# Signalling the rotated differential queries and keys to TensorE in two parts instead of one

## The chip, the cores and the metric

The kernel runs on one core of one Trainium2 chip. The metric is the device time of one launch in microseconds (us). Three runs of the kernel before gave 2773.07, 2773.71 and 2776.54 us; the median is 2773.71 us.

The engines are called PE (TensorE, matrix products and transposes), PEld (its weight loads), DVE (VectorE), ACT (ScalarE), POOL (GpSimd) and SP (SyncE, which issues most DMAs).

## What is computed

Two blocks of two layers each work on a sequence of 512 rows of 1024 features. Only the first block is touched. In each of its layers a normed input `h` is multiplied with one wide matrix and cut into seven parts, of which `dq` and `dk` are the queries and keys of the differential attention:

```python
h = rmsnorm(x, g_mix[l])
dq, dk, dv, c_q, c_kv_kr, xq, gate_logits = jnp.split(h @ w_in[l], split_idx, axis=-1)
...
def diff_attention(q, k, v, ...):
    q = q.reshape(B, S, DIFF_HEADS, 2, DIFF_HEAD_DIM)      # 8 heads, 2 maps, 64 wide
    k = k.reshape(B, S, DIFF_HEADS, 2, DIFF_HEAD_DIM)
    q = rotary(rmsnorm(q, q_gain), c, s_)
    k = rotary(rmsnorm(k, k_gain), c, s_)
    o = causal_block_attention(q, k, v, DIFF_HEAD_DIM ** -0.5)
```

`dq` and `dk` are 1024 columns each. After the norm and the rotation they are needed with the features on the partitions, so the kernel turns them on TensorE (a transposition by a product with the identity). Beside the differential attention a layer has a latent attention (`mla`, fed by `c_q` and `c_kv_kr`) and an attention over a memory (`cross`), then gates, an output product and a feed-forward part.

## The kernel before

All products are in 32-bit floats and are made from parts: every weight slab of 128 rows is split into a high and a low part, and a product is three passes (high by high, low activations by high weights, high activations by low weights). SP loads the slabs into a ring of four. POOL writes the high part of a slab (line 371) and then the low part (line 374) into one of two places (`weight_parts`); for a few projections ACT writes the high parts (line 382). A place comes free when TensorE has used the slab that was in it. TensorE's product of a projection is `project`: for each slab it waits for the high part, makes two passes, waits for the low part, and makes the third (line 460 where the output has tokens on the partitions). Four matmuls are one pass. Every engine works through its own list in the order in which it is written; nothing is reordered.

The eight banks of PSUM are two halves of four, used in turn by the projections. `turn` (line 485) makes transposes into the half that the projection around it doesn't use, after the half has been emptied.

The columns of `dq` and `dk` are handled in four groups of 512 columns, called 0 to 3: `dq0`, `dq1`, `dk0`, `dk1`. For each group DVE does `products` (sums of squares at line 1381, the scaling at 1454, the four products with the rotation tables at 1458 to 1462, the reciprocal at 1466) and `sums` (the two sums at 1470 and 1471, the scaling with the norm at 1473, and a drain). Groups 0 and 1, and then group 2, are rotated while `dq1` to `dk1` are projected. Then DVE takes part in the eight units of the cross attention (`A.steps(0, U1, ...)`), and only behind these it rotates group 3. After group 3 comes a drain that raises the semaphore `diff_roped` once (line 1504).

On TensorE the eight cross units are woven into the projections `dk1` and `lat0`. Then comes the projection `lat1`: eight slabs of 336 columns. Ahead of its slabs 1, 3, 5 and 7 it calls `turn_diff(0)` to `turn_diff(3)`, which turn groups 0 to 3 into `d_t0` to `d_t3`, 16 transposes each. All four wait for `diff_roped` to be 1. `d_t0` also needs the half of PSUM that `lat0` filled; ACT empties that (line 1193). After each turn ACT copies the bank half to `qkt`, and the next turn waits for that copy.

After `lat1` come `dv0` (with two turns of the latent part in it), the small projections `qb0` to `kvb1`, `dv1`, and then the 32 units of the differential attention. DVE's next work after group 3 is the low parts of the turned latent rows (line 600), and later the rotation and norms of the latent attention (from line 1536).

Of the kernel before, what the change touches and what calls it, by code (L numbers as in the profile page):

```python
# [877 lines left out]
def block_one(nc, io, m, s, layer, prev):  # L878
# [106 lines left out]
    for p2 in range(CH // 2):  # L985
        for i in (0, 3, 1, 2):
# [3 lines left out]
                              v=[(lambda kb, h=h: mv[:, kb, h * CHD:(h + 1) * CHD]) for h in hh]))  # L990
    for h in range(DH):
        for i in (0, 3, 1, 2):
            units.append(dict(kind="diff", pair=h, i=i, n=(i + 1) * P, mask=(m["causal16"][:], i * P),
                              q=[qkt[r, h, i * P:(i + 1) * P] for r in halves], k=[qkt[r, 8 + h, 0:(i + 1) * P] for r in halves],
                              v=[(lambda kb, h=h: dv[:, kb, h * P:(h + 1) * P])], scaled=len(units) - U1 + 1, joined=lam_neg))
    for p2 in range(MH // 2):
        for i in (0, 3, 1, 2):
# [3 lines left out]
                              v=[(lambda kb, h=h: vm[:, kb, h, :]) for h in hh], first=True, last=True, bank=6 + p2 % 2,  # L1001
# [39 lines left out]
    if True:  # L1041
# [21 lines left out]
        def _(pe):  # L1063
# [34 lines left out]
                L.turn(pe, f"lat_t{k}", [(c % 4, t * P, lat_chunk(t, c)) for c in chunks for t in range(TT)])  # L1098

            def turn_diff(k):  # L1100
                pe.wait_ge(s["diff_roped"], 1)
                L.turn(pe, f"d_t{k}", [(c, t * P, qk[:, t, (4 * k + c) * P:(4 * k + c + 1) * P]) for c in range(4) for t in range(TT)])

            L.project(pe, "dq1", ht, {4: turn_xq, 6: turn_mk})
            L.project(pe, "dk0", ht)
            L.attend(pe, A, 0, U1, ("dk1", ht), ("lat0", ht), every=2)
            L.project(pe, "lat1", ht, {1 + 2 * k: lambda k=k: turn_diff(k) for k in range(4)})
            L.project(pe, "dv0", ht, {2: lambda: turn_latent(0), 4: lambda: turn_latent(1)})
            L.emptied(pe, "lat_t1")
# [249 lines left out]
        def _(dve):  # L1359
            v = nc.vector  # L1360
# [122 lines left out]
            A.maximum(0)  # L1483
            A.maximum(1)
            turning_of[2][1]()

            def finish(u):
                a = units[u]
                dve.wait_ge(s["weighted"], u + 1)
                r = m["recip"][:, u % 8, :]  # L1490
                v.reciprocal(r, m["rowsum"][:, u % 8, :])
                v.drain()
                sums = ps[:, 6 + u % 2, 0:2 * P]
                i, p2 = a["i"], a["pair"]
                if a["kind"] == "cross":
                    v.tensor_tensor(oc[:, i, 2 * p2 * P:2 * (p2 + 1) * P].rearrange("p (j d) -> p j d", j=2),
                                    sums.rearrange("p (j d) -> p j d", j=2), bc(r, [P, 2, P], 2),
                                    ALU.mult).then_inc(s["finished"], 1)
                    return
# [648 lines left out]
```

## Time and profile before

| what | value |
|---|---|
| device time, median of 3 runs | 2773.71 us |
| device time, lowest and highest | 2773.07 and 2776.54 us |
| span of the profiled execution, first to last instruction | 2772.1 us |
| mean granted TensorE clock | 0.980 of full speed |
| PE busy | 2606.5 us, 94% of the span |
| POOL busy | 1947.2 us, 70% |
| DVE busy | 1093.7 us, 39% |
| ACT busy | 770.6 us, 28% |

The profile is of one execution; the device time of that very execution is not among the three listed, and the median of the runs is 1.6 us above the profile's span. A busy share is an average over the whole program. The part that matters here is short: from about 208 us to 245 us of the span in the first layer, and the same stretch from about 1258 us in the second. Times in a row are from the start of the span. In a row of the timeline, "[8.37 <-DVEq L1504]" says that the engine was idle for 8.37 us before the row and that DVE's queue, at line 1504, ended the idle time. Rows merge equal instructions that follow each other, and the busy time of a merged row of matmuls overlaps the next row a little, so durations of stretches are taken from one start to the next.

### The profile page before, as it was taken

To read this page: it belongs to the slowest core of one execution; us is meant where nothing else is said; L and a number is where in the kernel's file an instruction comes from. 1 tells how busy PE (TensorE), PEld (TensorE's weight loads), DVE (VectorE), ACT (ScalarE), POOL (GpSimd) and SP (SyncE) were. 2 spreads that over 40 slices of the span, in tenths; PEclk is the share of its full clock that TensorE was granted. 3 is DMA by queue.
4 is the path that set the end of the run, shared out by engine and by line. 5 is a ranking of instruction groups with operands and counts; after the bars stand their busy time and mean duration, and the time that the engine had idled before them with its cause. 6 is when DMAs were issued, how large, how long until landed. Compare 5 with 4: busy or idle time off the path is not lost. (4 is left out here: it accounts for less than half of the span.)

```text
span 2772.1 us, 35631 instructions
## 1 busy us (share of the span) xinstructions
PE 2606.5 (94%) x13648; PEld 2108.8 (76%) x13652; DVE 1093.7 (39%) x1710; ACT 770.6 (28%) x1517; POOL 1947.2 (70%) x1604
## 2 busy tenths in 40 slices
PE   5998899999999999998899999999998997989987
PEld 4887677877878887787677878888887975688756
DVE  3544773111220112544674211210102399536883
ACT  4332474100120112342374100120111233313251
POOL 4646704888898888746803888898896878277844
PEclk9999999999999999999999999999999998999989
DMA  4322201333333333322201333233333431043202
GB/s 134 97 62 68 62 1 39 91 95 92 107 91 96 96 97 114 95 67 67 73 1 31 88 94 92 92 95 96 95 99 78 107 81 34 28 96 90 75 1 76
DMA packets 159257, 214.49 MB, mean 77 GB/s; under 512 B 51696, under 2 KB 69360, under 8 KB 159088
## 3 DMA queue, kind: packets, MB, share of 16 engines
q1 hardware_dynamic: 120336, 207.27, 25.7%
q10 hardware_dynamic: 38752, 4.95, 1.3%
q8 instruction: 109, 1.79, 0.3%
q14 instruction: 60, 0.49, 0.1%
HBM read 210.06 MB, written 2.10 MB: 77 GB/s over the span
## 5 line engine op out<-in xcount | busy, mean ns | idle before, releaser
L371 POOL TENSOR_TENSOR weight_parts<-weight_ring,zero 128x512 fp32r<-128x512 f32 (+4 forms) x730 | 789.2, 1081 | 667.9 <-PE ps L462 351.8
L374 POOL TENSOR_TENSOR weight_parts<-weight_ring,weight_parts 128x512 fp32r<-128x512 f32 (+3 forms) x804 | 1059.0, 1317 | 136.0 <-ACT weight_parts L382 77.9
L462 PE MATMUL ps<-h_feature_major_high,weight_parts 128*128 128x512 f32 x2304 | 588.9, 394 | 9.7 <-POOL weight_parts L371 9.4
L462 PEld LDWEIGHTS ps<-h_feature_major_high,weight_parts 128*128 128x128 f32 x2304 | 428.2, 188 | 115.7 <-POOL weight_parts L371 16.9
L460 PE MATMUL ps<-weight_parts,h_feature_major_high 128*128 128x512 f32 (+3 forms) x1904 | 429.4, 363 | 20.5 <-POOL weight_parts L371 7.8
L460 PEld LDWEIGHTS ps<-weight_parts,h_feature_major_high 128*128 128x128 f32 x1904 | 333.4, 189 | 72.9 <-POOL weight_parts L371 11.3
L462 PE MATMUL ps<-h_feature_major_low,weight_parts 128*128 128x512 f32 x1152 | 309.7, 391 | 0.0
L460 PE MATMUL ps<-weight_parts,ut_high 128*128 128x512 f32 x1008 | 251.6, 390 | 1.1 <-POOL weight_parts L371 0.9
L462 PEld LDWEIGHTS ps<-h_feature_major_low,weight_parts 128*128 128x128 f32 x1152 | 217.4, 189 | 46.0
L460 PE MATMUL ps<-weight_parts,h_feature_major_low 128*128 128x512 f32 (+3 forms) x952 | 227.3, 361 | 0.0
L460 PEld LDWEIGHTS ps<-weight_parts,ut_high 128*128 128x128 f32 x1008 | 188.3, 188 | 43.6 <-POOL weight_parts L374 2.2
L460 PEld LDWEIGHTS ps<-weight_parts,h_feature_major_low 128*128 128x128 f32 x952 | 169.8, 189 | 22.5
L825 ACT ACTIVATE probs<-ps,negmax 128x256 f32<-128x256 f32 (+3 forms) x320 | 164.2, 522 | 78.2 <-DVE negmax L811 77.2
L701 PE MATMUL ps<-arena 64*128 64x256 f32 (+8 forms) x640 | 154.7, 484 | 29.0 <-ACT probs L825 19.4
L1636 DVE TENSOR_TENSOR ut_low<-outs,ut_high 128x2048 fp32r<-128x2048 f32 x16 | 45.6, 2852 | 319.0 <-ACT ut_high L1355 319.0
L811 DVE TENSOR_REDUCE negmax<-ps 128x2 f32<-128x512 f32 (+3 forms) x160 | 129.2, 808 | 85.4 <-PE ps L706 62.2
L1351 ACT ACTIVATE outs<-ps 128x2048 f32<-128x2048 f32 x16 | 30.1, 1884 | 405.4 <-PE ps L462 405.4
L460 PE MATMUL ps<-weight_parts,ut_low 128*128 128x512 f32 x504 | 134.8, 389 | 0.0
L462 PE MATMUL ps<-ot_high,weight_parts 128*128 128x512 f32 x512 | 128.1, 389 | 0.0
L1326 ACT ACTIVATE arena<-ps,small 128x512 f32<-128x512 f32 x48 | 29.1, 689 | 319.8 <-PE ps L462 319.8
L701 PEld LDWEIGHTS ps<-arena 64*128 64x128 f32 (+2 forms) x640 | 67.6, 194 | 64.5 <-ACT probs L825 26.7
L462 PEld LDWEIGHTS ps<-ot_high,weight_parts 128*128 128x128 f32 x512 | 96.1, 188 | 19.9
(297 smaller groups left out, 3057.4 us busy)
## 6 DMA issues: line engine op xcount, KB each, us to landing
weight_ring<-in_w_in SPq DMA_DIRECT2D x272, 256.0 KB, 2.6
weight_ring<-in_w_mlp SPq DMA_DIRECT2D x256, 256.0 KB, 2.6
weight_ring<-in_w_out SPq DMA_DIRECT2D x64, 256.0 KB, 2.7
weight_ring<-in_w_mem_kv SPq DMA_DIRECT2D x32, 256.0 KB, 2.7
weight_ring<-in_w_diff_o SPq DMA_DIRECT2D x32, 256.0 KB, 2.6
weight_ring<-in_w_in SPq DMA_DIRECT2D x32, 170.0 KB, 2.3
weight_ring<-in_w_in SPq DMA_DIRECT2D x32, 168.0 KB, 2.2
weight_ring<-in_w_in SPq DMA_DIRECT2D x32, 163.0 KB, 2.2
```

The lines of the kernel that those rows point to most:

```text
L371: self.nc.gpsimd.tensor_tensor(high, raw, self.m["zero"][:].broadcast_to([P, raw.shape[1]]), ALU.add).then_inc(self.s["slab_high"], 1)
L374: self.nc.gpsimd.tensor_tensor(low, raw, high.bitcast(F32), ALU.subtract).then_inc(self.s["slab_split"], 1)
L460: last = self.nc.tensor.matmul(banks[:, t, 0:width], h[:, cut], w, **ends)
L462: last = self.nc.tensor.matmul(banks[:, t, :], w[:, cut], h, **ends)
L701: last = pe.matmul(bank[:, 0:a["n"]], a["q"][j], a["k"][j], start=True, stop=a["mask"] is None)
L811: last = dve.tensor_reduce(out, self.m["ps"][:, 2 * (u % 2):2 * (u % 2) + 2, 0:a["n"]], AX.X, ALU.max, negate=True)
L825: last = act.activation(self.m["probs"][:, u % 3, j, 0:a["n"]], self.m["ps"][:, 2 * (u % 2) + j, 0:a["n"]], ACT.Exp, bias=self.m["negmax"] ...
L1326: last = a.activation(gates[k % 2][:, j, :], L.banks(name)[:, j, :], ACT.Sigmoid, bias=bgate[:, ch:ch + 1])
L1351: a.activation(r, L.banks(f"up{f}{j}"), ACT.Relu)
L1636: v.tensor_tensor(ut[1][:, 4 * j:4 * j + 4, :], rect[(f * ups + j) % 2], ut[0][:, 4 * j:4 * j + 4, :].bitcast(F32), ALU.subtract).then_inc ...
```

## The change

The wait of the first three turns is unchanged in number, the wait of the fourth becomes 2, and DVE gets one more drain with a raise of the semaphore directly behind the rotation of group 2. So the first raise now says that groups 0 to 2 are done, and the old raise, behind group 3, is the second. No arithmetic, no transfer and no buffer is changed, and the order of work on every engine stays as it was. The change stands once in the code and works in both layers of the first block.

```diff
             def turn_diff(k):
-                pe.wait_ge(s["diff_roped"], 1)
+                pe.wait_ge(s["diff_roped"], 1 if k < 3 else 2)
                 L.turn(pe, f"d_t{k}", [(c, t * P, qk[:, t, (4 * k + c) * P:(4 * k + c + 1) * P]) for c in range(4) for t in range(TT)])
...
             A.maximum(0)
             A.maximum(1)
             turning_of[2][1]()
+            v.drain().then_inc(s["diff_roped"], 1)
 
             def finish(u):
```

## Rows read from the trace of the kernel before

**Rows 1.** The page, busy time and share of each engine.

```profile
PE 2606.5 (94%) x13648; PEld 2108.8 (76%) x13652; DVE 1093.7 (39%) x1710; ACT 770.6 (28%) x1517; POOL 1947.2 (70%) x1604
```

**Rows 2.** Line 1504: its drains, and who waited for them (us, times).

```profile
L1504 DVEq DRAIN  x2: 19/19/19, 221.0 to 1270.6; - x2
...
  PEld ps L485: 17.3, 2
```

**Rows 3.** PE timeline, first layer: start, us, engine, line, operation [idle before <-releaser].

```profile
211.77 0.89 PE L460 MATMUL ps<-weight_parts,h_feature_major_high 128*128 128x336 f32 x4 [0.27 <-POOL weight_parts L374]
221.03 3.68 PE L485 MATMUL ps<-ident,arena 128*128 128x128 f32 x16 [8.37 <-DVEq L1504]
...
229.06 1.91 PE L485 MATMUL ps<-ident,arena 128*128 128x128 f32 x16
230.72 0.86 PE L460 MATMUL ps<-weight_parts,h_feature_major_high 128*128 128x336 f32 x4
...
234.50 1.91 PE L485 MATMUL ps<-ident,arena 128*128 128x128 f32 x16
```

**Rows 4.** PE timeline, the same place in the second layer.

```profile
1261.38 0.89 PE L460 MATMUL ps<-weight_parts,h_feature_major_high 128*128 128x336 f32 x4 [0.27 <-POOL weight_parts L374]
1270.65 3.68 PE L485 MATMUL ps<-ident,arena 128*128 128x128 f32 x16 [8.38 <-DVEq L1504]
...
1277.91 0.82 PE L485 MATMUL ps<-ident,arena 128*128 128x128 f32 x6
```

**Rows 5.** ACT timeline: `lat0` is emptied.

```profile
209.94 1.30 ACT L1193 ACTIVATE probs<-ps 128x1344 f32<-128x1344 f32 x1 [1.52 <-PE ps L460]
```

**Rows 6.** DVE timeline, first layer.

```profile
177.58 0.69 DVE L811 TENSOR_REDUCE negmax<-ps 128x2 f32<-128x512 f32 x1 [6.43 <-PE ps L701]
...
211.03 1.77 DVE L1461 TENSOR_TENSOR arena<-arena,small 128x1024 f32<-128x1024 f32 x1
...
216.24 1.76 DVE L1471 TENSOR_TENSOR arena<-arena,outs 128x1024 f32<-128x1024 f32 x1
218.08 2.82 DVE L1473 TENSOR_TENSOR arena<-arena,small 128x2048 f32<-128x2048 f32 x1
252.15 2.73 DVE L600 SCALAR_TENSOR_TENSOR latt_low<-ps,small,latt_high 128x512 fp32r<-128x512 f32 x4 [31.25 <-ACT latt_high L593]
...
320.22 0.43 DVE L811 TENSOR_REDUCE negmax<-ps 128x2 f32<-128x256 f32 x1 [9.34 <-PE ps L706]
```

**Rows 7.** POOL timeline, slabs 1 to 3 of `lat1`, first layer.

```profile
211.68 1.72 POOL L371 TENSOR_TENSOR weight_parts<-weight_ring,zero 128x336 fp32r<-128x336 f32 x1
213.48 1.76 POOL L374 TENSOR_TENSOR weight_parts<-weight_ring,weight_parts 128x336 fp32r<-128x336 f32 x1
215.20 1.72 POOL L371 TENSOR_TENSOR weight_parts<-weight_ring,zero 128x336 fp32r<-128x336 f32 x1
217.00 1.75 POOL L374 TENSOR_TENSOR weight_parts<-weight_ring,weight_parts 128x336 fp32r<-128x336 f32 x1
227.53 0.75 POOL L371 TENSOR_TENSOR weight_parts<-weight_ring,zero 128x336 fp32r<-128x336 f32 x1 [8.77 <-PE ps L460]
228.35 0.92 POOL L374 TENSOR_TENSOR weight_parts<-weight_ring,weight_parts 128x336 fp32r<-128x336 f32 x1
```

**Rows 8.** DVE timeline, group 1 of the rotation, first layer.

```profile
143.97 3.22 DVE L1473 TENSOR_TENSOR arena<-arena,small 128x2048 f32<-128x2048 f32 x1
```

**Rows 9.** POOL timeline beside rows 8.

```profile
145.81 2.52 POOL L374 TENSOR_TENSOR weight_parts<-weight_ring,weight_parts 128x512 fp32r<-128x512 f32 x1 [0.78 <-ACT weight_parts L382]
148.53 1.29 POOL L374 TENSOR_TENSOR weight_parts<-weight_ring,weight_parts 128x512 fp32r<-128x512 f32 x1 [0.20 <-ACT weight_parts L382]
```

**Rows 10.** Windows: length, busy us of PE, PEld, DVE, ACT, POOL, then clock.

```profile
212.60:221.00 8.40, 0.06 (x1) 0.00 (x0) 8.15 (x6) 0.00 (x0) 6.00 (x4) 0.71 0.22 61
221.00:224.40 3.40, 3.37 (x17) 3.37 (x17) 0.00 (x0) 0.00 (x0) 0.00 (x0) 0.50 0.00 0
```

**Rows 11.** Windows: the start of the differential attention in both layers.

```profile
321.00:328.00 7.00, 4.01 (x29) 2.14 (x27) 6.02 (x12) 4.94 (x19) 7.00 (x6) 1.00 0.00 0
1370.00:1377.00 7.00, 5.03 (x28) 3.03 (x27) 6.38 (x12) 4.88 (x19) 7.00 (x5) 0.76 0.00 0
```

## The prediction, made before the changed kernel ran

> **What bounds the kernel now.** I read the page first: TensorE is busy 94% of the span [rows 1], so a time in which it stands still is a time that the program loses, unless something behind it is late anyway. Then the view of the line that raises the semaphore: TensorE's weight loads waited twice for line 1504, 17.3 us in all [rows 2]. Then TensorE's timeline around both waits. In the first layer the last pass of slab 0 of `lat1` starts at 211.77, and the first of the 16 transposes of `d_t0` only at 221.03, after 8.37 us of idle time that DVE's queue ended [rows 3]; in the second layer the same wait is 8.38 us [rows 4]. Last the timelines of the other engines in that stretch, to see what else TensorE would have had to wait for.
>
> **What the wait costs, with what follows it.** After the idle time TensorE runs at its lower level: the granted clock is 0.71 over the idle stretch and 0.50 (1.2 of 2.4 GHz) over the 3.4 us in which `d_t0` is made [rows 10]. So I don't take the idle time as the price but compare the stretch with an undisturbed one. At full clock, `d_t1` takes 230.72 - 229.06 = 1.66 us, and from its start to that of `d_t2` there are 234.50 - 229.06 = 5.44 us, so two slabs take 3.78, a slab 1.89 and a pass 0.63 [rows 3]. From the last pass of slab 0 to `d_t1` there would be 0.63 + 5.44 = 6.07 us without any wait. There are 229.06 - 211.77 = 17.29 in the first layer and 1277.91 - 1261.38 = 16.53 in the second [rows 3, 4] (the clock came back sooner there). Too much: 11.22 and 10.46, together 21.7 us.
>
> **What the change removes and adds.** Groups 0 to 2 were rotated before the cross attention, so their signal has long been given when TensorE comes to `d_t0`. What else must be there: the half of PSUM that `lat0` filled, which ACT has emptied at 209.94 + 1.30 = 211.24 [rows 5], before TensorE gets there at 211.77 + 0.63 = 212.40. So the first wait goes entirely. The fourth turn now waits for the second raise, at 218.08 + 2.82 = 220.9 in DVE's timeline [rows 6], and it comes to that place about 10 us later than this (below); that wait is free. The added drain stands between the rotation of group 2 and the cross attention. The drain of line 1504 takes 19 ns [rows 2], and DVE waits 6.43 us for TensorE soon after the new one [rows 6]; I take 0. Without that cover it would be some 0.02 us for each layer, or with a restart of DVE's pipeline up to the 0.08 us or so between its dependent rows, as 218.08 against 216.24 + 1.76 = 218.00 [rows 6].
>
> **What is late next: POOL.** While DVE rotates group 3, POOL is slow. Its two parts of a 336-column slab take 0.75 and 0.92 us alone, but 1.72 and 1.76 beside the rotation [rows 7]. These rows fit in a simple way: a POOL instruction that starts while a DVE instruction with two inputs runs stands until that one ends. Line 1461 ends at 211.03 + 1.77 = 212.80, and the high part begun at 211.68 ends at 213.40, 0.60 later; line 1471 ends at 218.00, and the low part begun at 217.00 ends at 218.75 [rows 6, 7]. In an earlier group it is the same: line 1473 ends at 147.19, and a low part that began at 145.81 ends at 148.33, 1.14 behind it, where one alone takes 1.29 [rows 8, 9]. Before the change this was hidden in TensorE's idle time: POOL filled both places and then waited 8.77 us for TensorE [rows 7]. Now TensorE meets it. Worked through for the first layer:
> - `d_t0` 212.40 to 214.06. Slab 1: its high part is ready at 213.40, two passes to 215.32; the low part at 213.48 + 1.76 = 215.24; third pass to 215.95. No wait.
> - Slab 2: high part ready at 215.20 + 1.72 = 216.92. Wait 0.97; two passes to 218.18. Low part at 218.75. Wait 0.57; end 219.38. `d_t1` 219.38 to 221.04.
> - Slab 3: POOL begins the high part at 218.83, inside line 1473 (218.08 to 220.90), so it ends at 220.90 + 0.60 = 221.50. Wait 0.46. The low part, alone now, is there at 221.58 + 0.92 = 222.50, before it is wanted. Slab 3 ends at 223.39, slab 4 at 225.28, and `d_t2` begins there.
> - From here POOL is ahead again: 1.67 us of work for a slab against 1.89 on TensorE and a turn besides.
>
> So `d_t2` begins at 225.28 in place of 234.50, 9.22 us earlier; that is 11.22 less the three waits, 2.00. `d_t3` would come at 230.7, 9.8 us behind the end of line 1473. In the second layer the gain is 10.46 - 2.00 = 8.46, if POOL and DVE stand to each other as in the first (TensorE's own rows do, to 0.01 us [rows 3, 4]). Sum: 17.7 us.
>
> The Trainium skill states such a rule, in "SBUF — State Buffer", section "SBUF: two separate sides": VectorE and GpSimd share a pair of ports under an exclusive lock, held for the whole instruction. That agrees with the rows just read. If it were a sharing of bandwidth, or if there were no contest at all, the three waits would be smaller or none, and the gain would be up to the 21.7 us from above; the rows are why I take 17.7.
>
> **Is it given back later?** All that follows is led by TensorE. DVE, after group 3, stands idle for 31.25 us and is released by ACT, which follows TensorE's turn; at the start of the differential attention DVE had waited 9.34 us for TensorE [rows 6]. The latent work between these two also starts from what TensorE has made, so it moves with it. POOL waits for TensorE behind the stretch [rows 7]. I find no step bound to a fixed time. So the whole gain should reach the end: span 2772.1 - 17.7 = 2754.4, and with the 1.6 us that lie between the span and the median of the runs, **2756.0 us**.
>
> **Rivals.**
> - *No contest between DVE and POOL that TensorE feels* (POOL gets ahead in some way that the old order hid). Gain 21.7, time 2752.0. For it: POOL had both places full in the old run. Against it: the ready times above are of exactly this stretch. 8%.
> - *The clock falls all the same.* TensorE now has three short waits, 2.0 us in 9. At the start of the differential attention, where it is busy 4 to 5 of 7 us, the clock stayed at 1.00 in the first layer and was 0.76 in the second [rows 11], so such a stretch can go either way. The price is at most what the low clock cost in the first layer: 11.22 less the idle time 221.03 - 212.40 = 8.63, so 2.59 us a layer, 5.2 in all. Time between 2756.0 and 2761.2; I put it at 2759. Against it: none of the three waits is over 0.97 us. 17%. The Trainium skill, in "TensorE: Matmul & The Clock Gate", section "A second HAM failure mode: psum-queue depth-cycling", tells of a kernel in which small idle times between groups of matmuls made the clock swing between its two levels; that is a rule against this change, and the second layer's attention agrees with it, the first's doesn't.
> - *The wait comes back further on*, at one of the joints (latent norms, POOL's slabs of `dv1`, DVE's chain before the attention). It would need a joint where something other than TensorE came last by nearly as much. All or most of 17.7 is lost: 2768 to 2774. The 9.34 us of slack at DVE's last joint speak against it. 5%.
> - *Slower.* One mechanism: TensorE falls to 1.2 GHz at the short waits in `lat1` and stays there until the last turn. From `d_t0` to the end of `d_t3` there are 18.0 us of work at full clock (four turns of 1.66, six slabs of 1.89), which would take 36. The loss of 18 a layer less the mean gain of 8.85 is 9.1, twice: 2773.7 + 18.3 = 2792 us. It decides from 8.85 us of work run at half clock in each layer. Against it: the clock came back within about 5 us of steady work after a far longer pause. 2%.
> - *The change doesn't do what it says*, since another signal of `d_t0` is late by as much as DVE. Only ACT's emptying is there, and it was done 9.8 us before `d_t0` began. No change, 2773.7. 3%.
>
> **How the numbers follow.** The forecast has 65%; its own range is 2754 to 2758 for the positions of DVE and POOL to each other, which decide 2.0 us a layer. With the rivals on both sides the range is 2752.0 to 2761.5, which leaves out the two that give no gain and the slower one. About 0.2% (5.5 us) is what a measurement of this kernel can tell from no change. Faster by more: 65 + 8 + 17 and a part of the third rival, 0.92. Within 0.2%: 0.05. Slower: 0.03.
>
> **What the profile after would show.** The line of the old wait no longer releases TensorE before `d_t0`; `d_t0` starts 0.6 us after the last pass of slab 0 and takes 1.66 us; three short waits for POOL at lines 371 and 374, of about 1.0, 0.6 and 0.5 us, follow; POOL's 8.77 us of idle time in this stretch is gone; the granted clock is 1.00 from 212 to 225. `d_t2` stands 9.2 us earlier than before, and the same distance is still there at the start of the differential attention and of the second layer, and 17.7 at the end. I am wrong if `d_t0` still waits, if these waits sum to far more than 2 us, or if the distance shrinks between `lat1` and the attention.

## The result: 2755.4 us, 18.7 us faster

The changed kernel takes 2755.36 us (median of 4 runs, 2754.26 to 2756.41) against 2774.05 us (4 runs); the ratio is 0.9930 with a 95% interval of 0.9918 to 0.9942. Timed again on one chip with three of the experiments it took 2755.66 us against 2776.13 us, 20.5 us less, ratio 0.9927 (0.9915 to 0.9940). The forecast was 2756.0 us, a gain of 17.7 us. The first interval covers gains from about 16 to 23 us, so the times alone can't tell 17.7 from 21.7; the traces have to. The profiled execution spans 2753.2 us, with a mean granted clock of 0.983 (0.980 before), and its own device time was 2755.17 us.

First the place of the old wait, in TensorE's timeline of the changed kernel (start us, us, engine, line, operation, [idle before <-releaser]); it answers to [rows 3]:

```profile
212.02 0.89 PE L460 MATMUL ps<-weight_parts,h_feature_major_high 128*128 128x336 f32 x4 [0.28 <-POOL weight_parts L374]
212.75 1.91 PE L485 MATMUL ps<-ident,arena 128*128 128x128 f32 x16
214.41 0.86 PE L460 MATMUL ps<-weight_parts,h_feature_major_high 128*128 128x336 f32 x4
...
217.25 0.88 PE L460 MATMUL ps<-weight_parts,h_feature_major_high 128*128 128x336 f32 x4 [0.74 <-POOL weight_parts L371]
217.97 0.78 PE L460 MATMUL ps<-weight_parts,h_feature_major_low 128*128 128x336 f32 x4
219.09 0.88 PE L460 MATMUL ps<-weight_parts,h_feature_major_high 128*128 128x336 f32 x4 [0.35 <-POOL weight_parts L374]
219.81 1.91 PE L485 MATMUL ps<-ident,arena 128*128 128x128 f32 x16
221.84 0.89 PE L460 MATMUL ps<-weight_parts,h_feature_major_high 128*128 128x336 f32 x4
...
225.63 1.91 PE L485 MATMUL ps<-ident,arena 128*128 128x128 f32 x16
...
231.07 1.91 PE L485 MATMUL ps<-ident,arena 128*128 128x128 f32 x16
```

`d_t0` now follows the last pass of slab 0 at once, and takes 214.41 - 212.75 = 1.66 us. Two waits for POOL are marked, and the third shows as a gap: `d_t1` begins at 219.81, should end at 221.47, and slab 3 begins at 221.84. From the last pass of slab 0 to `d_t2` there are 225.63 - 212.02 = 13.61 us, against 22.73 before. The second layer is the same:

```profile
1252.56 0.89 PE L460 MATMUL ps<-weight_parts,h_feature_major_high 128*128 128x336 f32 x4 [0.29 <-POOL weight_parts L374]
...
1266.18 1.91 PE L485 MATMUL ps<-ident,arena 128*128 128x128 f32 x16
```

It has 13.62 us, against 21.96 before: the last pass of slab 0 at 1261.38, `d_t1` at 1277.91 [rows 4], and 5.43 more to `d_t2`, which that trace has at 1283.34. So the stretch is shorter by 9.12 and 8.34 us, 17.5 in all.

POOL's timeline (to hold against [rows 7]) shows what TensorE meets:

```profile
215.47 1.72 POOL L371 TENSOR_TENSOR weight_parts<-weight_ring,zero 128x336 fp32r<-128x336 f32 x1
217.27 1.77 POOL L374 TENSOR_TENSOR weight_parts<-weight_ring,weight_parts 128x336 fp32r<-128x336 f32 x1
219.00 2.79 POOL L371 TENSOR_TENSOR weight_parts<-weight_ring,zero 128x336 fp32r<-128x336 f32 x1
221.87 0.91 POOL L374 TENSOR_TENSOR weight_parts<-weight_ring,weight_parts 128x336 fp32r<-128x336 f32 x1
222.74 0.74 POOL L371 TENSOR_TENSOR weight_parts<-weight_ring,zero 128x336 fp32r<-128x336 f32 x1
```

The high part of slab 3 takes 2.79 us in place of 0.75. DVE's line 1473 (in its own timeline) is why, and DVE's idle times further on show that nothing took the time back:

```profile
218.35 2.83 DVE L1473 TENSOR_TENSOR arena<-arena,small 128x2048 f32<-128x2048 f32 x1
243.28 2.73 DVE L600 SCALAR_TENSOR_TENSOR latt_low<-ps,small,latt_high 128x512 fp32r<-128x512 f32 x4 [22.10 <-ACT latt_high L593]
...
311.37 0.42 DVE L811 TENSOR_REDUCE negmax<-ps 128x2 f32<-128x256 f32 x1 [9.34 <-PE ps L706]
```

Line 1473 ends at 221.18 and POOL 0.61 later. DVE's idle time before the latent rows shrank from 31.25 to 22.10 us, that is by 9.15, nearly the 9.12 by which the stretch on TensorE became shorter, and its slack at the start of the attention is 9.34 as before [rows 6]. The windows of [rows 10] have the full clock now (length, busy us of PE, PEld, DVE, ACT, POOL, clock, DMA share, GB/s):

```profile
212.60:221.00 8.40, 7.31 (x53) 6.73 (x53) 8.25 (x6) 1.89 (x1) 8.24 (x5) 1.00 0.23 61
221.00:224.40 3.40, 3.28 (x23) 3.04 (x22) 0.18 (x1) 1.88 (x1) 3.24 (x4) 1.00 0.16 37
```

### The profile page after: what moved, and what is told of

It reads as the page before. It is cut to its first block and busy times, and to the rows that moved or that the text cites. A ratio compares the mean times of both kernels' runs of the same rounds, so it can differ in the third digit from the quotient of the medians.

```text
span 2753.2 us, 35633 instructions
## 1 busy us (share of the span) xinstructions
PE 2604.8 (95%) x13648; PEld 2103.9 (76%) x13652; DVE 1092.2 (40%) x1710; ACT 771.1 (28%) x1517; POOL 1954.1 (71%) x1604
```

## The experiments

| kernel | median us | runs | ratio to before, 95% interval |
|---|---|---|---|
| the raise alone | 2774.55 | 11 | 1.000 (0.9991 to 1.0009) |
| before, wait filled | 2769.47 | 11 | 0.998 (0.9972 to 0.9989) |
| changed, second turn waits | 2760.36 | 5 | 0.995 (0.9937 to 0.9962) |
| changed, ACT's highs in `lat1` | 2752.37 | 4 | 0.992 (0.9907 to 0.9934) |
| changed, again | 2755.66 | 5 | 0.9927 (0.9915 to 0.9940) |
| changed, third turn waits | 2755.94 | 5 | 0.9927 (0.9914 to 0.9939) |
| before, ACT's highs in `lat1` | 2772.84 | 11 | 0.9986 (0.9977 to 0.9995) |
| changed, ACT's highs in `lat1` and `dv1` | 2746.32 | 4 | 0.9893 (0.9879 to 0.9906) |

The first four ran beside 21 runs of the kernel before (median 2774.14 us), the others beside 15 (2776.13 us).

**The raise alone.** The edit on the changed kernel:

```diff
-                pe.wait_ge(s["diff_roped"], 1 if k < 3 else 2)
+                pe.wait_ge(s["diff_roped"], 2)
```

> The changed kernel with all four turns waiting for the second raise, so the added drain and raise stand alone and the wait is back. My theory (the added drain is free, the gain is the wait alone): 2774 us, ratio to before 1.000, TensorE again idle for 8.4 us in each layer before d_t0. Rival (the drain or the raise itself changes something, for instance the cross units behind it): a time off 2774 by more than 2 us.

Measured 2774.55 us, ratio 1.000, and the wait is back in TensorE's timeline:

```profile
221.70 3.57 PE L485 MATMUL ps<-ident,arena 128*128 128x128 f32 x16 [8.38 <-DVEq L1505]
```

So the added drain and raise cost nothing that can be measured (the interval is 2.5 us wide on either side), and the gain is that of the earlier signal.

**The wait filled.** The kernel before, where TensorE turns the identity 76 times into the banks of `d_t0` ahead of the wait; the results of these are written over. The lines left out below are the 16 transposes of `d_t0` itself, as before.

```diff
             def turn_diff(k):
+                if k == 0:
+                    L.begin(pe, "d_t0")
+                    dst = L.banks("d_t0")
+                    for i in range(76):
+                        pe.transpose(dst[:, i % 4, 0:P], ident[:], ident[:])
+                    pe.wait_ge(s["diff_roped"], 1)
...
+                    last.then_inc(s["banks_full"], 1)
+                    return
                 pe.wait_ge(s["diff_roped"], 1)
```

> The kernel before, with 76 idle transposes of the identity (about 7.9 us at full clock) ahead of the wait of d_t0; the wait stays. It separates the idle time from the low clock that follows it. My theory (of 21.7 us, 4.4 are the low clock after the wait: 2.6 in the first layer and 1.8 in the second): about 2769.6 us, d_t0 takes 1.66 us in place of 3.33, ratio 0.998. Rival (the clock has no part, all of it is idle time): 2774 us.

Measured 2769.47 us, 4.7 us under the kernel before, ratio 0.998 with an interval that leaves out 1. TensorE's timeline:

```profile
212.13 0.89 PE L460 MATMUL ps<-weight_parts,h_feature_major_high 128*128 128x336 f32 x4 [0.29 <-POOL weight_parts L374]
212.86 8.46 PE L1105 MATMUL ps<-ident 128*128 128x128 f32 x76
221.42 1.97 PE L1109 MATMUL ps<-ident,arena 128*128 128x128 f32 x16
223.14 0.86 PE L460 MATMUL ps<-weight_parts,h_feature_major_high 128*128 128x336 f32 x4
```

And the window in which `d_t0` was made at half clock before:

```profile
221.00:224.40 3.40, 3.30 (x27) 3.06 (x26) 0.28 (x1) 0.98 (x1) 0.00 (x0) 1.00 0.02 5
```

The turn takes 223.14 - 221.42 = 1.72 us at full clock in place of 3.33. From the last pass of slab 0 to `d_t1` (at 226.91) there are 14.78 us, 2.51 less than in [rows 3]; in the second layer 1.76 less. Work that nobody needs, put into a wait, gained 4.3 us: that much of the old loss was the low clock behind the wait, and not the wait itself.

**The second turn waits.**

```diff
-                pe.wait_ge(s["diff_roped"], 1 if k < 3 else 2)
+                pe.wait_ge(s["diff_roped"], 1 if k < 1 else 2)
```

> The changed kernel, but the second turn (group 1) already waits for the second raise. It wants to start at about 219.8 and the raise comes at 221.2, while POOL has slab 3 ready only at 221.8 anyway. My theory (what comes after is bound by POOL until slab 3): d_t1 waits 1.4 us, slab 3 then needs no wait (0.4), so the loss is about 1.0 us a layer and 2.0 us in all: 2757.4 us. Rival (any wait on this path costs in full, with a falling clock): 1.4 us and up to 2.6 more in each layer, 2758 to 2763 us.

Measured 2760.36 us, 3 us more than my theory gave and within the rival's 2758 to 2763. In the profile `lat1` did what my theory said: `d_t1` waits 1.35 us for DVE, slab 3 no longer waits for POOL, and `d_t2` starts 14.08 us after `d_t0`, 1.20 more than in the changed kernel, in both layers.

```profile
221.67 1.97 PE L485 MATMUL ps<-ident,arena 128*128 128x128 f32 x16 [1.35 <-DVEq L1505]
```

The attention behind it took 119.7 us in the first layer in place of 118.4, with the clock at 0.74 from 312 to 322. A second profile of the same kernel:

> One more profile of the kernel whose second turn waits for the second raise. Its timed median was 2760.4 us where I expected 2757.4; its profile shows 1.2 us a layer in lat1, as expected, and an attention of 119.7 us in place of 118.4 in the first layer, with a low clock at its start. My theory (the low clock at the start of the attention comes and goes): again 1.2 us a layer in lat1, and attentions of 118.4 or of 119.5 to 120.5 us in either layer. Rival (the wait in lat1 has a further price in lat1 itself): over 1.5 us a layer there.

This profile shows the rival's price in one of its two layers:

```profile
222.37 3.22 PE L485 MATMUL ps<-ident,arena 128*128 128x128 f32 x16 [1.34 <-DVEq L1505]
225.23 1.35 PE L460 MATMUL ps<-weight_parts,h_feature_major_high 128*128 128x336 f32 x4
```

After the same wait of 1.34 us `d_t1` takes 2.86 us here, and the granted clock was 0.60 on average from 222.3 to 225.2, so TensorE ran at its lower level for most of it, and `d_t2` starts 229.49 - 213.79 = 15.70 us after `d_t0`, 1.6 us more than in the first profile. In one of four passes through this stretch, then, the clock fell within it; in the changed kernel's three profiles, six passes, it never did. My theory holds for the wait itself and had left out the clock; how much of the 3 us each of the two places of low clock makes in the timed runs is open.

**The third turn waits.** `1 if k < 2 else 2`.

> The changed kernel, but the third turn (group 2) already waits for the second raise. It wants to start at 225.6, the raise comes at 221.2. My theory (slack of 4.4 us): the same time as the changed kernel within 1 us, so a split of two and two groups would do as well. Rival (a change of the waits by itself moves the time by several us, as the 2.9 us of the kernel whose second turn waits, over my expectation of 2757.4, may suggest): 2 us or more off the changed kernel.

Measured 2755.94 us beside 2755.66 of the changed kernel. The slack of the second raise is as large as read; signalling two groups and two would have done as well.

**ACT writes some high parts in `lat1`.** The edit, on the changed kernel:

```diff
-    L.high_by_act = set(highs_mem) | {...}
+    lat1 = L.slab_at["lat1", 0]
+    L.high_by_act = set(highs_mem) | {...} | {lat1 + k for k in (1, 2, 3)}
...
+            L.write_slab_highs(act, [lat1 + 1, lat1 + 2])
             for k in range(4):
                 empty(f"d_t{k}", qkt[:, 4 * k:4 * k + 4, :])
+                if k == 0:
+                    L.write_slab_highs(act, [lat1 + 3])
```

> The changed kernel, with the high parts of slabs 1, 2 and 3 of lat1 written by ACT in place of POOL, so POOL has half the work in the stretch in which DVE's rotation stops it. My theory (the three waits of 2.0 us a layer are POOL locked out by DVE): the waits for POOL in slabs 1 to 3 go or fall under 0.3 us, gain 1.6 to 2.0 us a layer, about 2751.8 us. Rival (the waits come from the slab transfers, or ACT's part collides with emptying d_t0): no gain, 2755 us, or slower.

Measured 2752.37 us. The waits are gone; TensorE's timeline:

```profile
212.02 0.88 PE L460 MATMUL ps<-weight_parts,h_feature_major_high 128*128 128x336 f32 x4 [0.28 <-POOL weight_parts L374]
...
218.18 1.91 PE L485 MATMUL ps<-ident,arena 128*128 128x128 f32 x16
...
223.61 1.91 PE L485 MATMUL ps<-ident,arena 128*128 128x128 f32 x16
```

223.61 - 212.02 = 11.59 us, which is 2.02 less than in the changed kernel; in the second layer it is 2.03. The three waits of the prediction are therefore worth what it said. In the time it is 3.0 us under the changed kernel, but the two intervals overlap and the two kernels were timed in different sets, so this step by itself is shown by the traces and not by the timing.

**The same on the kernel before.**

> The kernel before (one raise), with the high parts of slabs 1 to 3 of lat1 written by ACT as in the kernel that gained 3 us on the changed one. My theory (in the kernel before POOL's slowness lies within TensorE's wait for DVE): no gain here, 2774 us, within 1 us. Rival (ACT's part is worth 3 to 4 us by itself): 2770 us.

Measured 2772.84 us against 2776.13, ratio 0.9986 (0.9977 to 0.9995): a gain of 3.3 us, by the interval between 1.4 and 6.4, where I had said none. The trace shows why. TensorE waits less for DVE (TensorE's timeline):

```profile
220.06 3.49 PE L485 MATMUL ps<-ident,arena 128*128 128x128 f32 x16 [7.45 <-DVEq L1508]
```

DVE's timeline in the same profile:

```profile
216.35 1.21 DVE L1475 TENSOR_TENSOR arena<-arena,outs 128x1024 f32<-128x1024 f32 x1
217.64 2.29 DVE L1477 TENSOR_TENSOR arena<-arena,small 128x2048 f32<-128x2048 f32 x1
```

POOL's timeline:

```profile
209.91 5.43 POOL L374 TENSOR_TENSOR weight_parts<-weight_ring,weight_parts 128x336 fp32r<-128x336 f32 x3
```

The second sum and the scaling took 1.76 and 2.82 us in [rows 6], beside POOL. Without high parts POOL had run out of work by 215.34, so DVE ran alone. TensorE's wait is 8.37 - 7.45 = 0.92 us shorter in the first layer and 0.93 in the second, 1.85 of the 3.3 us; the rest isn't assigned. The hindrance goes both ways: DVE holds up POOL, and POOL holds up DVE. My reading had only the first. The rows of the changed kernel above show the same from DVE's side: its line 1473 starts at 218.35, inside POOL's low part, which ends at 217.27 + 1.77 = 219.04, and it ends 2.14 us behind that, where it takes 2.29 alone. Each of the two engines, then, seems to stand until the other's instruction is over and then to run at its own speed.

**ACT's high parts also in `dv1`.** Further on, TensorE waits for line 371 in four slabs of `dv1`, in the first layer of the changed kernel 1.16, 0.85, 0.87 and 0.87 us. ACT is idle there. The edit, on the kernel with ACT's highs in `lat1`:

```diff
-    ... | {lat1 + k for k in (1, 2, 3)}
+    ... | {lat1 + k for k in (1, 2, 3)} | {dv1 + k for k in (1, 2, 3, 4)}
...
+            L.write_slab_highs(act, [dv1 + k for k in (1, 2, 3, 4)])
             roots(st_both)
```

> The changed kernel with ACT writing the high parts of slabs 1 to 3 of lat1 and also of slabs 1 to 4 of dv1, where TensorE waits for POOL's line 371 by 1.16, 0.85, 0.87 and 0.87 us in each layer while DVE squares the latent queries and keys. My theory (the same lock, and ACT is idle there): these four waits fall to under 0.5 us in all, 3.3 us a layer, some 6.5 us less than with lat1 alone: 2746 us. Rival (the attention behind dv1 starts when DVE's chain is done, so the time comes back as a wait for DVE; or the waits only move to POOL's low parts): 2752 us.

Measured 2746.32 us, as expected, ratio 0.9893 (0.9879 to 0.9906), beyond the interval of the changed kernel beside it. Of the four waits one is left; TensorE's timeline in the first layer:

```profile
285.40 1.21 PE L460 MATMUL ps<-weight_parts,h_feature_major_high 128*128 128x512 f32 x4 [0.41 <-ACT weight_parts L382]
286.45 1.09 PE L460 MATMUL ps<-weight_parts,h_feature_major_low 128*128 128x512 f32 x4
287.38 1.99 PE L460 MATMUL ps<-weight_parts,h_feature_major_high 128*128 128x512 f32 x8
```

DVE's slack before the attention has fallen from 9.34 to 5.06 us, so this joint doesn't take the time back yet. This is the fastest kernel of the study, 9.3 us under the changed one.

**The changed kernel and the kernel before, further profiles.**

> The changed kernel once more, beside the next three on one chip, to have them compared directly. 2755.4 us, ratio 0.993, in every theory.

> One more profile of the changed kernel. My theory: lat1 as before (d_t2 starts 12.9 us after d_t0), attentions of 118.4 us or, where the clock falls at their start, up to 120.5 us. Rival (the changed kernel never has that low clock): 118.4 us in both layers, as in its two profiles so far.

> One more profile of the kernel before, for the stretches of low clock outside lat1. In the first profiles the changed kernel gained 1.5 us between the end of the second layer's attention (1486.4 against 1469.3) and its last turn of x (1779.4 against 1760.8). My theory (whether the clock falls after a short pause differs from execution to execution, and this has nothing to do with the change): from the last line 701 of the second layer to the last line 1140 there are 291.5 to 293.3 us in either kernel, and the two lengths occur in both. Rival (the change shortens it): 293.0 us in every profile of before.

In all three profiles of the changed kernel the last transpose of the four turns starts 19.9 to 20.0 us after the first, and the attentions last 118.3 to 118.4 us in both layers. So do those of the kernel before in its two profiles, though the clock fell at their start at least once (0.76 in [rows 11]), and in the second profile of the changed kernel too (0.88 from 309 to 319). In the first profile of each of the seven other kernels one attention or both lasted 119.1 to 120.7 us; why none of the five profiles of these two kernels has this is open. From the last matmul of the second layer's attention scores (line 701) to the last transpose of `x` behind it (line 1140) the changed kernel took 291.5, 293.2 and 291.6 us, the kernel before 293.0 and 293.2. The shorter length goes with a full clock from 1485 to 1520, the longer with a mean of 0.95; the first profile of the changed kernel has this window:

```profile
1485.00:1520.00 35.00, 32.65 (x160) 27.16 (x160) 11.20 (x12) 10.58 (x16) 27.50 (x22) 1.00 0.27 76
```

and the second this:

```profile
1485.00:1520.00 35.00, 32.65 (x152) 26.98 (x153) 10.21 (x11) 10.66 (x16) 26.38 (x20) 0.95 0.26 73
```

The same kernel shows both lengths. The kernel before shows only the longer, in two profiles. But the kernel with the raise alone, which waits for DVE as the kernel before does, took 291.5 us in its profile, with the full clock:

```profile
1485.00:1520.00 35.00, 32.55 (x207) 25.13 (x206) 12.33 (x20) 11.60 (x23) 18.20 (x13) 1.00 0.14 39
```

So the shorter length doesn't need the wait to be gone, and the 1.5 us between the lengths are no part of what the change gives by its mechanism.

## Why the prediction was right

**The wait goes, and nothing else stood behind it.** Right, and shown from both sides: with the raise alone the wait and the time of before are back; with it split, `d_t0` starts 0.73 us after the last pass (the prediction said 0.63; a pass that follows a wait is 0.1 us longer).

**The price is more than the idle time.** Right. By the prediction's numbers 4.4 us of the 21.7 are the low clock (11.22 and 10.46 less the idle 8.63 in each layer); filling the wait gained 4.3 in the traces and 4.7 in the time.

**POOL is late next, by 2.00 us a layer.** Right in size: 2.02 and 2.03 us, by the kernel in which ACT takes over the high parts. The three waits were put at 0.97, 0.57 and 0.46; the same differences of starts give 0.91, 0.51 and 0.37 for the two marked ones and the gap, with short restarts beside them. The rule in the Trainium skill ("SBUF — State Buffer", section "SBUF: two separate sides"), an exclusive lock held for a whole instruction, agrees with these rows: POOL's high part of slab 3 ended 0.61 us behind DVE's line 1473, which had still 2.18 us to run when it began, and in [rows 6, 7] another ended 0.60 us behind line 1461, which had 1.12 to run.

**The added drain is free.** Right: 1.000 with the raise alone.

**The second raise has 9.8 us of slack at the fourth turn.** Right. `d_t3` starts at 231.07, the drain of line 1505 is at 221.2, and even the third turn can wait for it.

**Nothing is given back.** Right. The distance was 8.9 us at the first layer's attention (319.5 against 310.6), 17.1 at the second's (1368.0 against 1350.9), and 18.9 at the end of the span. The working gives 17.7 and `lat1` alone 17.5; 1.5 us of the rest lie behind the second attention, in the stretch whose length changes with the clock. That part is luck of the profiled execution: the kernel with the raise alone has the shorter length too. The medians gave 18.7 us in one set and 20.5 in the other, 1.0 and 2.8 us above the forecast; how much of this is such luck or the spread of the runs, and how much a low clock made rarer by the change, is open. The forecast time lies 0.6 us from the measured one; the runs themselves spread over 2.2 us, so that closeness is in part luck too.

**The rivals.** No contest with POOL (2752.0) is refuted by the waits seen, which went when ACT took over the high parts; the times alone would not have refuted it. The falling clock didn't occur in `lat1` of the changed kernel, but the kernel with one further wait of 1.35 us had it in one pass of four; it deserved its place. The slower case, a clock that stays low, was not seen: the turn behind the fall above took 2.86 us, and the second pass after it was at full clock again.

## What to carry to other kernels

When one signal covers several pieces of work that finish at different times, look at which piece the first waiter needs; if the work that releases it was done long ago, split the signal and price the gain from a start before the wait to a start after the engine is steady again, since the low clock behind a pause of TensorE is part of the loss. Then walk the producer that feeds the freed engine: here GpSimd had used the pause to make up for VectorE's interference, and its lateness took 2 us of 11. Where GpSimd splits weights while VectorE works with operands in SBUF, see whether ScalarE is idle: here it took half of GpSimd's work on three slabs over and gave the 2 us back, and with four more slabs at another place the kernel came 9.3 us under the changed one.

## What was not expected of the hardware

- The contest between POOL and DVE slows both. DVE's second sum and its scaling of group 3 lost 0.55 (1.76 against 1.21) and 0.53 us (2.82 against 2.29) to POOL's weight splitting, in a stretch where TensorE waited for DVE.
- 76 useless transposes in a wait of 8.4 us made the kernel 4.7 us faster.
- The same wait of 1.35 us was followed by a turn of 1.7 us at full clock in three passes and by one of 2.86 us in the fourth, within one kernel. A length that is right in one profile can be off by 1.6 us in the next, from the clock alone.
